# A latent attention layer's query sums: squares folded onto one head's rows by transfers and additions, and one sum product for two heads

## The reference, cut to what matters

```python
q = (rms_norm(cq, q_norm_g) @ w_uq).reshape(B, S, C_HEADS, QK_HEAD)   # 8 heads, 192 wide
...
q = rms_norm(q, qn_g)          # mean of the squares over 192 features, for each token and head
k = rms_norm(k, kn_g)
...
o = block_causal_attention(q, k, v).reshape(B, S, C_WIDTH) * jax.nn.silu(z)
return x + o @ w_out
```

## Time and profile before

| | |
|---|---|
| median of the runs | 2616.68 us |
| the profiled execution's own time | 2616.89 us |
| its span, first to last instruction | 2615.1 us |
| PE busy | 2598.9 us, 99% of the span |
| PEld busy | 2121.3 us, 81% |
| DVE busy | 1419.4 us, 54% |
| ACT busy | 1023.5 us, 39% |
| POOL busy | 235.5 us, 9% |
| the 64 records of the query sum products (L2687 on `q_sq`) | 7.8 us |

### The profile page before, as it was taken

How to read it: one execution, slowest core, us unless ns; L and a number is a source line. 1 busy time by engine, 2 the same in 40 slices (tenths; PEclk the granted TensorE clock), 3 DMA queues, 4 the chain that set the end, 5 groups by cost and what they waited for, 6 DMA issues and landing times.

```text
span 2615.1 us, 33021 instructions
## 1 busy us (share of the span) xinstructions
PE 2598.9 (99%) x12318; PEld 2121.3 (81%) x12318; DVE 1419.4 (54%) x1863; ACT 1023.5 (39%) x1592; POOL 235.5 (9%) x173
## 2 busy tenths in 40 slices
PE   8999999999999999999999999999999999999999
PEld 7888887878888888888887778888887888888877
DVE  5444248875444335444258765444236657845773
ACT  4222135654222223222136644222235554334663
POOL 0000024201000010000034101000001110012220
PEclk9999999999999999999999999999999999999999
DMA  4222223113222223222232112222222222322221
GB/s 165 96 96 96 96 99 103 65 41 105 96 96 96 96 81 113 96 96 96 96 108 92 59 58 97 96 96 96 97 97 73 81 87 85 107 97 93 85 73 53
DMA packets 70323, 239.13 MB, mean 91 GB/s; under 512 B 8528, under 2 KB 10832, under 8 KB 70224
## 3 DMA queue, kind: packets, MB, share of 16 engines
q1 hardware_dynamic: 69792, 236.91, 26.9%
q10 hardware_dynamic: 432, 0.87, 0.1%
HBM read 230.15 MB, written 2.10 MB: 89 GB/s over the span
## 4 chain that ended last, share of the span: by engine, by line
PE 93%; DVE 3%; issue 2%; ACT 1%; DVEq 1%; POOL 0%; DMA 0%; POOLq 0%; ACTq 0%; SPq 0%
PE bank L419 20%; PE bank L421 20%; PE bank L420 20%; PE score L419 5%; PE score L420 5%; PE score L421 5%; PE flip_bank L419 2%; PE flip_bank L420 2%; PE flip_bank L421 2%; PE score L1182 1%; PE flip_bank L1210 1%; PE score L2742 1%; PE bank L2777 1%; PE score L1923 1%; PE bank L1232 1%
## 5 line engine op out<-in xcount | busy, mean ns | idle before, releaser
L393 DVE TENSOR_TENSOR w_lo<-w_raw,w_hi 128x1024 fp32r<-128x1024 f32 x425 | 526.8, 1241 | 543.7 <-ACT w_hi L353 532.7
L419 PE MATMUL bank<-h_hi,w_hi 128*128 128x512 f32 x1840 | 733.6, 399 | 1.1 <-DVE w_lo L393 1.1
L421 PE MATMUL bank<-h_hi,w_lo 128*128 128x512 f32 x1840 | 717.4, 390 | 0.0
L420 PE MATMUL bank<-h_lo,w_hi 128*128 128x512 f32 x1840 | 716.5, 389 | 0.0
L353 ACT ACTIVATE w_hi<-w_raw 128x1024 fp32r<-128x1024 f32 x427 | 447.2, 1051 | 385.6 <-DMA w_raw<-stream 385.3
L419 PEld LDWEIGHTS bank<-h_hi,w_hi 128*128 128x128 f32 x1840 | 345.9, 188 | 75.1 <-issue 5.0
L421 PEld LDWEIGHTS bank<-h_hi,w_lo 128*128 128x128 f32 x1840 | 345.3, 188 | 73.0
L420 PEld LDWEIGHTS bank<-h_lo,w_hi 128*128 128x128 f32 x1840 | 346.1, 188 | 71.2 <-issue 2.4
L553 ACT ACTIVATE hid_hi<-tmp 128x512 f32 (+1 forms) x88 | 55.6, 632 | 408.6 <-DVE tmp L778 408.6
L772 DVE TENSOR_TENSOR tmp<-bank,rstd 128x512 f32<-128x512 f32 x132 | 91.1, 691 | 148.4 <-PE bank L421 148.1
L548 ACT ACTIVATE tmp<-tmp 128x512 f32<-128x512 f32 x88 | 55.6, 632 | 248.9 <-DVE tmp L772 248.9
(11 more groups left out here) (536 smaller groups left out, 3831.7 us busy)
## 6 DMA issues: line engine op xcount, KB each, us to landing
w_raw<-stream SPq DMA_DIRECT2D x427, 512.0 KB, 3.2
tmp<-tmp SPq DMA_DIRECT2D x64, 64.0 KB, 2.0
x_tok<-x SPq DMA_DIRECT2D x4, 512.0 KB, 6.3
wx_raw<-stream SPq DMA_DIRECT2D x4, 512.0 KB, 4.7
out<-out_tok SPq DMA_DIRECT2D x8, 256.0 KB, 2.0
tmp<-qr SPq DMA_DIRECT2D x16, 64.0 KB, 2.5
tab_in_f<-tables SPq DMA_DIRECT2D x1, 704.0 KB, 10.5
cos_sin<-rope ACTq DMA_DIRECT2D x1, 512.0 KB, 4.7
```

The source lines that it names most:

```text
L393: nc.vector.tensor_tensor(w_lo[:, s, :], w_raw[:, s, :], w_hi[:, s, :].bitcast(F32), ALU.subtract).then_inc(lo_ready, 1)
L419: nc.tensor.matmul(dst, whi, xhi, start=start, stop=False)
L420: nc.tensor.matmul(dst, whi, xlo, start=False, stop=False)
L421: return nc.tensor.matmul(dst, wlo, xhi, start=False, stop=stop)
```

## The change

ACT now issues, behind each head's square and copy, a DMA that moves the half of `q_sq` in which the rotary rows do not lie onto the other 64 partitions, into `folded`. That is no new buffer but the columns 256 to 511 of `c_probs`' second buffer: head 0 of the pair lies on its partitions 0 to 63 and head 1 on 64 to 127. GpSimd adds, behind its two old additions, the other half of each head (L2231 of the new kernel), so that each head's sum over features is one over 64 partitions. PE then has four products for two heads, with the two columns of the table `halves`, which holds ones in rows 0 to 63 and in rows 64 to 127.

```diff
+        folded = c_probs[:, 1, :, 2 * P:4 * P]
...
 # GpSimd, query_squares(u)
                 for j in range(2):
                     pool.wait_ge(q_evac, 2 * u + j + 1)
                     rows = slice(HEAD * j, HEAD * j + HEAD)
-                    ins = nc.gpsimd.tensor_tensor(q_sq[rows, j, :], q_sq[rows, j, :], rope_sq[rows, u % 2, :], ALU.add)
+                    nc.gpsimd.tensor_tensor(q_sq[rows, j, :], q_sq[rows, j, :], rope_sq[rows, u % 2, :], ALU.add)
+                pool.drain()
+                pool.wait_ge(q_moved, 32 * (u + 1))
+                for j in range(2):
+                    rows = slice(HEAD * j, HEAD * j + HEAD)
+                    ins = nc.gpsimd.tensor_tensor(folded[rows, :, :], folded[rows, :, :],
+                                                  q_sq[rows, j, :].rearrange("p (a n) -> p a n", a=2), ALU.add)
                 ins.then_inc(q_added, 1)
...
 # ScalarE, queries(u), for j in range(2)
                     nc.scalar.activation(q_sq[:, j, :], src, ACT.Square)
                     nc.scalar.activation(qn[:, u % 2, j, :], src, ACT.Copy, scale=col("qn_nope")).then_inc(q_evac, 1)
+                    rows, other = slice(HEAD * j, HEAD * j + HEAD), slice(HEAD - HEAD * j, P - HEAD * j)
+                    act.wait_ge(q_evac, 2 * u + j + 1)
+                    if u >= 2 and j == 0:
+                        act.wait_ge(c_flipped, TB * (u - 1))
+                    act.dma_start(folded[rows, :, :], q_sq[other, j, :].rearrange("p (a n) -> p a n", a=2)).then_inc(q_moved, 16)
...
 # VectorE, query_sums(u)
-                src = c_bank("qsum", u)
+                src = c_bank("qsum", u)[:, 0:2 * TB].rearrange("p (b j) -> p j b", j=2)
                 for j in range(2):
-                    ins = nc.vector.tensor_tensor(q_inv(u)[:, j, :], src[:, TB * j:TB * j + TB], cq_mean, ALU.add)
+                    ins = nc.vector.tensor_tensor(q_inv(u)[:, j, :], src[:, j, :], cq_mean, ALU.add)
...
 # TensorE, query_sums(u)
-            def query_sums(u, j):
-                dst = c_bank("qsum", u) if j else fresh("qsum", u)
-                if j == 0:
-                    pe.wait_ge(q_added, u + 2)
+            def query_sums(u):
+                dst = fresh("qsum", u)
+                pe.wait_ge(q_added, u + 2)
                 for b in range(TB):
-                    ins = column(dst, TB * j + b, b, q_sq[:, j, :])
-                if j == 1:
-                    ins.then_inc(q_summed, 1)
+                    ins = nc.tensor.matmul(dst[:, 2 * b:2 * b + 2], folded[:, b // 2, P * (b % 2):P * (b % 2) + P],
+                                           table("halves", 2), start=True, stop=True)
+                ins.then_inc(q_summed, 1)
...
 # TensorE, the unit (z, 1), ahead of the first softmax step
-                    dense("z", 1, 0, 4)
-                    query_sums(0, 0)
-                    dense("z", 1, 4, 5)
-                    query_sums(0, 1)
-                    dense("z", 1, 5, KT)
+                    dense("z", 1, 0, KT)
+                    query_sums(0)
...
 # TensorE, the z unit at b = 2
-                        query_sums(u + 1, 0)
                         dense(kind, t, 0, 1)
-                        query_sums(u + 1, 1)
+                        query_sums(u + 1)
                         dense(kind, t, 1, 4)
```

More of the change, by code:

```diff
@@ L2174, in build @@
         q_summed, q_sums_in = sem("q_summed"), sem("q_sums_in")
+        q_moved = sem("q_moved")
         k_ready = sem("k_ready")
```

## The result

The changed kernel takes 2627.24 us, the median of seven runs between 2625.37 and 2634.83; the kernel before took 2617.27 beside it (seven runs, 2616.57 to 2620.34). The ratio is 1.0038 with a 95% interval of 1.0028 to 1.0047: slower by some 10 us. The forecast was 2620.5 in a range of 2614.9 to 2623.9. The sign was right, the size was not, and the time lies outside the range.

The account below looks back on a forecast made before the run. TensorE was taken as the bound, 93% of the chain. Losses net of savings, 1.25 + 0.6 + 1.1 + 0.85 = 3.8 us, on 2616.89 gave 2620.7, forecast as 2620.5 us since that execution is 0.2 above the median; range 2614.9 to 2623.9.

Parts of the forecast that it names:

- the one at the head: Whole kernel: TensorE is 93% of the chain, so only its work and its waits count.
- Pair 0: Scores start at 2431.5 instead of 2430.24, behind transfer, additions and rotation: 1.25 us lost, the saved group included.
- Pair 1: Key copy 0.75 us late, 0.84 saved, a new 0.7 us wait for the second key squares: 0.6 us lost.
- Pairs 2 and 3: ACT waits for transposes and issues transfers, delaying key copies; 1.1 us lost at pair 2, 0.85 at pair 3.
- The saving: One of two sum groups per pair goes, 0.84 us each, 3.4 us off TensorE over four pairs.
- The rival of a dear second column: Two-column products take twice as long, so the 3.4 us are not saved: 2623.9 us, chance 0.05.
- The issue: On ACT, starting each transfer holds the engine 0.59 us, with 0.35 as the other end.
- The rival of cheap issues: Issues cost ACT next to nothing, 0.05 us each: 2614.8 us, chance 0.10.
- The landing: Transfers land 2.3 us after the issue, between 1.9 and 3.8.
- the rival of late landing: Transfers beside weight loads land at 3.8 us, costing more at pairs 0 and 1: 2622.6 us, chance 0.17.
- The friction at pair 0: GpSimd's additions beside VectorE's rotation take 3.65 us; `q_added` comes at 2429.9, `roped` at 2431.4.
- Pair 1's key squares: GpSimd's additions end at 2443.8, the key-square chain takes 7.4 us to 2451.2; TensorE waits 0.7, between 0 and 1.3.

Follow-up runs that it names:

- the filled kernel: Changed kernel with products of no use put in TensorE's waits at pairs 0 to 3: 2623.83 us, ratio 1.0025 to the kernel before.
- all pairs: Changed kernel with rows of its own as the transfers' destination and SP issuing them, at all four pairs: 2624.66 us, ratio 1.0026 to the kernel before.
- pairs 1 to 3: Kernel before with the change at pairs 1, 2 and 3 only, rows of their own, SP issuing: 2619.92 us, ratio 1.0008.
- the shared rows: Changed kernel's destination in the probabilities' buffer, against the same kernel with rows of its own (2623.78 us), which is 3.1 us less over before.
- the sum products alone: Kernel before with one two-column sum group per pair, on the first head's squares, no transfer or new addition: 2614.56 us, ratio 0.9987.
- pairs 2 and 3 alone: Kernel before with the change at pairs 2 and 3 only, rows of their own, SP issuing: 2615.95 us, ratio 0.9991.
- the repeat: The changed kernel run again without edit, against the kernel before: 2627.01 us, ratio 1.0039.
- the kernel with its own rows: Changed kernel with the transfers going into rows of their own, no wait for the transposes, ACT still issuing: 2623.78 us, ratio 1.0022 to the kernel before.

## Why the prediction was wrong

The step that failed is the one at the head: "a microsecond counts only where PE does less, or where PE comes to wait". Each wait was priced at its length. A wait also makes the clock fall, and PE's products behind it are longer. Filling the waits shows that this is worth 3.2 us of the median's 9.5, and the windows count 10.2 us of it in the longest execution. No rival had it, and the range, built from waits alone, could not reach 2627; the filled kernel, without the clock's part, lies at 2623.8, just inside it.

The second failure is in the sizes, at the two places where GpSimd stands ahead of PE. Place by place, from the differences between kernels against their own runs of before; what is measured so holds the clock's part too:

| Place | predicted | measured | from |
|---|---|---|---|
| Pair 0 | +1.25 | +5.1 | all pairs (+7.3) less pairs 1 to 3 (+2.2), SP's issue |
| Pair 1 | +0.6 | +4.0 | pairs 1 to 3 (+2.2) less pairs 2 and 3 (-1.8), SP's issue |
| Pairs 2 and 3 | +1.95 | +1.3 | -1.8, and +3.1 for the shared rows (ACT's issue) |

- **The saving: right.** 0.84 us a pair; the sum products alone gave 2.9 of 3.4 (2.6 against those executions of before whose mean clock is 1.000, and 0.7 was given back in waits), pairs 2 and 3 alone 1.8 of 1.7. The rival of a dear second column falls with the 251 ns.
- **The issue: right in length, overpriced in effect.** 0.60 us measured, 0.59 taken. At pair 1 its 0.75 was measured as 0.7. But SP's issue, which takes it off ACT, gained nothing in the whole kernel; at pairs 2 and 3 it is free without the wait for the transposes. The rival of cheap issues falls all the same.
- **The landing: mis-sized.** 2.9 us in place of 2.3 (2.7 in the repeat's profile); at pair 0 the addition began 3.67 us after the end of the second copy (2425.19 to 2428.86), where I had 2.5, and between 3.1 and 4.2 us in the profiles of the repeat, the filled kernel and the kernel with its own rows. There the rival of late landing, with its 3.8 us, was nearer than the forecast. With the additions' 3.44 us (3.65 taken) `q_added` came 0.9 us later than predicted, at 2432.30, less 1.48 is 2430.8.
- **The friction at pair 0: half seen.** I took VectorE's rotation to end at 2431.4; it ended at 2432.85, less 1.48 is 2431.4. That was exact. But the scores stand behind the sums, which began at 2432.45, so they lost 2.19 us, not 1.25. Part of that is the clock already: from the sums' start to the scores it is 1.46 us here and 1.03 in the filled kernel (2430.30 to 2431.33).
- **Pair 1's key squares: mis-sized.** The additions ended at 2450.16, which is 2443.8 plus the shift there, as predicted. The chain of key squares behind them then took 8.7 us (2450.23 to 2458.94), where I had shortened 7.96 to 7.4. The "friction with VectorE that a later start partly escapes" was a guess with no row behind it: the chain grew by 0.8 us over the 7.96 in place of shrinking, and all of it sits in the second cast (L2215), 1.42 us where it took 0.61 before (L2212). The guess was wrong by 1.3 us, which is the whole miss: 2.0 us of wait in place of 0.7.
- **Pairs 2 and 3: right in mechanism, roughly right in size.** Waits of 2.50 and 1.79 us for 1.95 and 1.7. By the waits less the saving the two pairs lose 2.6 us, by the table 1.3; the forecast's 1.95 lies between, and the runs don't decide. At pair 2 the exponentials' idle time grew from 0.40 to 0.64 us instead of absorbing 0.15.

The three places add up to 10.4 us where the whole costs 9.5; the 0.9 between them is how SP's issue differs from ACT's in the whole kernel (7.3 and 6.4 over before, with rows of their own), and I leave it open. Of the miss of some 6 us the clock is 3.2 and the waits are 1.9 (5.7 in the repeat's profile for my 3.8); the rest of some 0.6 us is within what these medians can tell.

## What to carry to other kernels

Where TensorE is busy all the time, price a new wait on it at its length plus what the clock loses behind it; here that was a third of the damage, and it varied from run to run. A transfer and an addition that save products on TensorE bring their whole saving where the helper engine has room, and lose several times as much where its next work is already just in time: measure the room at each place and change only the places that have it. Don't sum parts measured alone, since they spend the same room; and a destination that is free only late can cost more than the transfer.

## What the runs showed of the hardware that was not expected

- TensorE's granted clock fell from 2.4 to 1.2 GHz behind waits of 1.8 to 3 us, and also behind a wait of 0.39 us beside two groups of one-column sum products, while it stayed up behind waits of 1.06 us (pair 1) and 0.83 us (the sum products alone); behind the same wait of 2.5 us it fell in one execution and not in the next. A profile at full speed is no promise that the next run has it.
- Useless products in a wait made the kernel 3.2 us faster, with nothing else changed.
- The issue of a transfer between SBUF rows held ACT 0.60 us with the destination in the probabilities' tile, and 0.47 with rows of its own (median of six); the landing was about the same, 2.9 and 2.8 us. Issued by SP into those rows it took 3.7 us.
- VectorE's operation on two SBUF operands (128 x 512) took 1.60 to 1.75 us beside GpSimd's additions, and 0.69 without.
